# Rotary half swap in a two-block transformer kernel: four small SBUF-to-SBUF DMAs per chunk in the place of a permutation product

## The reference

```python
def apply_rope(x, ang):
    cos = jnp.cos(ang)[None, :, None, :].astype(x.dtype)
    sin = jnp.sin(ang)[None, :, None, :].astype(x.dtype)
    x1, x2 = jnp.split(x, 2, axis=-1)
    return jnp.concatenate([x1 * cos - x2 * sin, x2 * cos + x1 * sin], axis=-1)

        h = rms_norm(x, norm_mix_pre[l])
        proj = h @ w_in[l]
        qa, ka, va, qb, kb, vb = jnp.split(proj, SPLITS, axis=-1)

        qa = apply_rope(rms_norm(qa.reshape(B, S, N_HEADS_A, HEAD_DIM), q_norm_a[l]), ang_axial)
        ka = apply_rope(rms_norm(ka.reshape(B, S, N_KV_A, HEAD_DIM), k_norm_a[l]), ang_axial)
        ...
        qb = apply_rope(qb.reshape(B, S, N_HEADS_B, HEAD_DIM), ang_1d)
        kb = apply_rope(kb.reshape(B, S, N_KV_B, HEAD_DIM), ang_1d)
```

## Time and profile before

| what | value |
|---|---|
| runs | 1419.41, 1420.99, 1421.65 us; median 1420.99 us |
| the profiled execution | 1421.76 us, its span 1420.0 us |
| busy over the span | PE 96%, DVE 49%, ACT 39%, POOL 10% |
| PE (TensorE matmul) on the chain that ended last | 89% |
| the stretch of the input projection and its rotations | about 24 to 99 us from the span's start |
| the attention's steps | from 98.93 us on |

### The profile page before, as it was taken

How to read it: one execution, slowest core, us unless ns; L and a number is a source line. 1 busy time by engine, 2 the same in 40 slices (tenths; PEclk the granted TensorE clock), 3 DMA queues, 4 the chain that set the end, 5 groups by cost and what they waited for, 6 DMA issues and landing times.

```text
span 1420.0 us, 14917 instructions
## 1 busy us (share of the span) xinstructions
PE 1366.1 (96%) x6184; PEld 1092.8 (77%) x6184; DVE 689.8 (49%) x890; ACT 547.2 (39%) x736; POOL 139.5 (10%) x132
## 2 busy tenths in 40 slices
PE   7988999999999999998999999999999999999995
PEld 5664668788888888886887777788888888888874
DVE  6998764644354442226434543465443544433244
ACT  6457864523232222224224454634332322232232
POOL 3441002400000001002000000002000000000012
PEclk9999999999999999998999999999999999999997
DMA  6210003122232222231321111123222322222311
GB/s 234 65 54 1 1 1 119 60 89 90 89 107 100 90 82 91 93 120 44 119 89 60 60 60 60 60 102 107 89 89 90 105 102 89 82 90 95 120 60 60
DMA packets 20595, 117.76 MB, mean 83 GB/s; under 512 B 2480, under 2 KB 2864, under 8 KB 9904
## 3 DMA queue, kind: packets, MB, share of 16 engines
q1 hardware_dynamic: 19392, 114.57, 23.4%
q10 hardware_dynamic: 1136, 2.24, 0.5%
HBM read 114.70 MB, written 2.10 MB: 82 GB/s over the span
## 4 chain that ended last, share of the span: by engine, by line
PE 89%; DVE 7%; DMA 1%; issue 1%; ACT 1%; POOL 0%; SPq 0%; POOLq 0%; DVEq 0%
PE ps L454 87%; PE ps L649 2%; DVE rt L1218 1%; DVE w_lo L1211 1%; DMA w_raw<-weights 1%; DVE nmax L1372 1%; DVE F L1215 1%; DVE X L1211 0%; ACT w_hi L819 0%; DVE rt L1211 0%; POOL sqsum L398 0%; DVE ps L1218 0%; DVE OUT L1218 0%; DVE h_lo L1218 0%; DVE y L1211 0%
## 5 line engine op out<-in xcount | busy, mean ns | idle before, releaser
L454 PE MATMUL ps<-h_hi,w_hi 128*128 128x512 f32 x1248 | 497.7, 399 | 20.8 <-DVE w_lo L1211 10.7
L454 PE MATMUL ps<-h_hi,w_lo 128*128 128x512 f32 x1248 | 488.5, 391 | 0.0
L454 PE MATMUL ps<-h_lo,w_hi 128*128 128x512 f32 x1248 | 488.4, 391 | 0.0
L1211 DVE TENSOR_TENSOR w_lo<-w_raw,w_hi 128x2048 fp32r<-128x2048 f32 (+2 forms) x117 | 246.5, 2110 | 256.7 <-ACT w_hi L819 256.6
L454 PEld LDWEIGHTS ps<-h_hi,w_hi 128*128 128x128 f32 x1248 | 235.8, 189 | 79.4 <-issue 15.0
L819 ACT ACTIVATE w_hi<-w_raw 128x2048 fp32r<-128x2048 f32 (+2 forms) x117 | 201.4, 1723 | 196.5 <-DMA w_raw<-weights 196.4
L454 PEld LDWEIGHTS ps<-h_lo,w_hi 128*128 128x128 f32 x1248 | 236.1, 189 | 51.0 <-issue 3.1
L454 PEld LDWEIGHTS ps<-h_hi,w_lo 128*128 128x128 f32 x1248 | 235.9, 189 | 49.7
L398 POOL TENSOR_TENSOR sqsum<-sqsum,sq 128x512 f32<-128x512 f32 x62 | 89.5, 1444 | 899.6 <-ACT sq L819 897.8
L454 PE MATMUL ps<-mid_hi,w_hi 128*128 128x512 f32 x352 | 136.9, 389 | 0.0
L454 PE MATMUL ps<-mid_lo,w_hi 128*128 128x512 f32 x352 | 136.9, 389 | 0.0
(11 more groups left out here) (179 smaller groups left out, 1239.4 us busy)
## 6 DMA issues: line engine op xcount, KB each, us to landing
w_raw<-weights SPq DMA_DIRECT2D x81, 1024.0 KB, 4.8
w_raw<-weights SPq DMA_DIRECT2D x32, 704.0 KB, 4.2
out_t<-OUT SPq DMA_DIRECT2D x8, 256.0 KB, 2.0
X<-x_t SPq DMA_DIRECT2D x3, 512.0 KB, 7.5
c<-constants ACTq DMA_DIRECT2D x1, 1280.0 KB, 9.5
w_raw<-weights SPq DMA_DIRECT2D x4, 256.0 KB, 8.1
wp_raw<-weights SPq DMA_DIRECT2D x1, 1024.0 KB, 8.0
X<-x_t SPq DMA_DIRECT2D x2, 256.0 KB, 4.0
```

Source lines behind the costliest of these rows:

```text
L454: return nc.tensor.matmul(out, lhsT, rhs, start=start, stop=stop, skip_group_check=loose)
L1211: return nc.vector.tensor_tensor(out, a, b, op)
```

## The change

Each chunk that is rotated (ten of the twelve) loses its permutation product. In its place, right behind the copy of the chunk to `y`, ScalarE's queue waits for that copy to end and issues four DMAs of 32 rows by 512 fp32 (64 KB each), from `y` to a row of `PP`, each to the place of the other half. `PP` is an SBUF tensor that is free until the attention is over; four of its rows are used in turn, each with its own semaphore. VectorE's `crossed` now reads and writes that SBUF row, where it read PSUM before; the signs are in the sine table. The items of the two value chunks (transposes) stay, and so do the sums of squares.

```diff
-        def rot_bank(j):
-            return 4 + j % 2 if j < LATE1 else 7 if j != 10 else 6
+        def turned(i):
+            return PP[:, 4 + i % 4, :]
...
             def item(j):
-                if j < 0:
-                    return
                 c = ORDER1[j]
-                if j < LATE1:
-                    free_item(j - 2)
-                elif j == 10:
-                    free_item(LATE1 - 1)
-                else:
-                    free_item({LATE1: LATE1 - 2, 11: LATE1}[j])
-                if j == 0:
-                    pe.wait_ge(c1_landed, 16)
-                pe.wait_ge(evac_act, EVAC["in1", j][1])
                 if c in V1:
+                    pe.wait_ge(evac_act, EVAC["in1", j][1])
                     for b in range(NB):
...
                     mm(ps[:, HSUM_BANK, :], c1[:, C_HONE - C1_AT:C_HONE - C1_AT + P], ysq[:, n % 2, :]
                        ).then_inc(hsum_done, 1)
-                mm(ps[:, rot_bank(j), :], c1[:, C_ROT - C1_AT:C_ROT - C1_AT + P], y_of(j)).then_inc(rot_done, 1)
...
-                if s in LATE_STEPS:
-                    item(LATE_STEPS[s])
+                if s == 9:
+                    item(11)
                 pe.wait_ge(pn_ready, s + 1)
-                if s == 0:
-                    free_item(LATE1 - 2)
-                if s == 1:
-                    free_item(LATE1 - 1)
...
                 af(y_of(j), ps[:, BANK["in1", j], :], ACT.Copy).then_inc(evac_act, 1)
+                if c not in V1:
+                    i = ROPED.index(c)
+                    act.wait_ge(evac_act, EVAC["in1", j][1])
+                    for to in range(0, P, HD // 2):
+                        at = to ^ HD // 2
+                        act.dma_start(turned(i)[to:to + HD // 2, :], y_of(j)[at:at + HD // 2, :]
+                                      ).then_inc(rot_landed[i % 4], 16)
...
-                straight, crossed = (rt if j < LATE1 else rt_late)[:, 0, :], (rt if j < LATE1 else rt_late)[:, 1, :]
+                straight, crossed = (rt if j < LATE1 else rt_late)[:, 0, :], turned(i_roped)
...
-                else:
-                    dve.wait_ge(rot_done, i_roped + 1)
+                dve.wait_ge(evac_act, EVAC["in1", j][1])
                 stt(straight, y_of(j), scale, c1[:, cos:cos + S], ALU.mult, ALU.mult)
-                dve.wait_ge(rot_done, i_roped + 1)
-                m = mark(stt(crossed, ps[:, rot_bank(j), :], scale_rot, c1[:, sin:sin + S], ALU.mult, ALU.mult))
+                dve.wait_ge(rot_landed[i_roped % 4], 64 * (i_roped // 4 + 1))
+                m = mark(stt(crossed, crossed, scale_rot, c1[:, sin:sin + S], ALU.mult, ALU.mult))
...
-    for m in range(P):
-        if m % HD < half:
-            c[m + half, C_ROT + m] = -1.0
-        else:
-            c[m - half, C_ROT + m] = 1.0
...
+        sign = np.where(i % HD < half, -1.0, 1.0)[:, None]
+        c[:, cos:cos + S], c[:, sin:sin + S] = np.cos(ang), sign * np.sin(ang)
```

More of the change, by code:

```diff
@@ L66 @@
 C1_AT = C_INVC + 4 * PADW
-C_HONE, C_ROT, C_MASK = C1_AT, C1_AT + P, C1_AT + 2 * P
-C_COSA, C_SINA, C_COSB, C_SINB = (C1_AT + 4 * P + S * i for i in range(4))
+C_HONE, C_MASK = C1_AT, C1_AT + P
+C_COSA, C_SINA, C_COSB, C_SINB = (C1_AT + 3 * P + S * i for i in range(4))
 C_COLS = C_SINB + S
@@ L223, in build @@
         dve_self, act_self, pool_self = sem("dve_self"), sem("act_self"), sem("pool_self")
-        ysq_ready, rot_done, hsum_done, hvar_ready, hguess_ready, rope_done, v_ready, eps_diag, eps_ready = (
-            sem(n) for n in ("ysq_ready", "rot_done", "hsum_done", "hvar_ready", "hguess_ready", "rope_done",
+        rot_landed = [sem(f"rot_landed{i}") for i in range(4)]
+        ysq_ready, hsum_done, hvar_ready, hguess_ready, rope_done, v_ready, eps_diag, eps_ready = (
+            sem(n) for n in ("ysq_ready", "hsum_done", "hvar_ready", "hguess_ready", "rope_done",
                              "v_ready", "eps_diag", "eps_ready"))
@@ L529, in _ @@
             KS = range(KD)
[L530 to L535, removed]
-                    else:
-                        pe.wait_ge(roped, ROPED.index(ORDER1[j]) + 1)
             def item(j):
-                if j < 0:
-                    return
                 c = ORDER1[j]
-                if j < LATE1:
-                    free_item(j - 2)
-                elif j == 10:
-                    free_item(LATE1 - 1)
-                else:
-                    free_item({LATE1: LATE1 - 2, 11: LATE1}[j])
-                if j == 0:
-                    pe.wait_ge(c1_landed, 16)
-                pe.wait_ge(evac_act, EVAC["in1", j][1])
                 if c in V1:
+                    pe.wait_ge(evac_act, EVAC["in1", j][1])
                     for b in range(NB):
-                        last = nc.tensor.transpose(ps[:, rot_bank(j), b * P:(b + 1) * P],
+                        last = nc.tensor.transpose(ps[:, SIDE_BANK if j else R_BANK, b * P:(b + 1) * P],
                                                    y_of(j)[:, b * P:(b + 1) * P], ident[:, :])
                     last.then_inc(vtr_done, 1)
-                    return
-                if c in NORMED:
+                elif c in NORMED:
                     n = NORMED.index(c)
@@ L561, in item @@
                         pe.wait_ge(hvar_ready, n)
+                    else:
+                        pe.wait_ge(c1_landed, 16)
                     pe.wait_ge(ysq_ready, n + 1)
@@ L579, in beside @@
                     factor(n_mix_pre)
-                for i in (0, 1) if j == 2 else (j - 1,) if j <= LATE1 else ():
+                for i in (0, 1) if j == 2 else (j - 1,) if 2 < j <= LATE1 else ():
                     item(i)
@@ L888, in finish @@
                     for b in range(NB):
-                        last = af((VA if c == 5 else VB)[:, b, :], ps[:, rot_bank(j), b * P:(b + 1) * P], ACT.Copy,
+                        last = af((VA if c == 5 else VB)[:, b, :], ps[:, SIDE_BANK if j else R_BANK, b * P:(b + 1) * P], ACT.Copy,
                                   scale=stat[:, 3, b:b + 1])
@@ L1595, in constants @@
         ang = np.concatenate([ang.astype(np.float32)] * 4).astype(np.float64)
-        c[:, cos:cos + S], c[:, sin:sin + S] = np.cos(ang), np.sin(ang)
+        sign = np.where(i % HD < half, -1.0, 1.0)[:, None]
+        c[:, cos:cos + S], c[:, sin:sin + S] = np.cos(ang), sign * np.sin(ang)
     for g, w in enumerate(POOL_WINDOWS):
```

## The result

| | before | after |
|---|---|---|
| median of the runs, us | 1420.63 (1419.41 to 1421.65, 4 runs) | 1431.09 (1429.34 to 1432.87, 4 runs) |
| profiled execution, and its span, us | 1421.76, 1420.0 | 1430.04, 1428.3 |
| ratio to before (95% interval) | | 1.0074 (1.0058 to 1.009) |
| first `nmax`, us from the start | 98.93 | 108.20 |

The change makes the kernel slower: by 10.5 us between the medians, by 8.3 us between the two profiled executions. In the profiles it is 9.3 us late when the attention starts. The median of before is over one execution more than the table ahead of the prediction has.

A forecast was written before the change was run, and what follows sets the result against it. VectorE mainly bounds the stretch up to the first nmax, TensorE the rest. +4.7 us at the attention's start (0.86 gain included), -0.7 for late products: +4.0 on 1421.76, or 1425.0 against the median; stated 1425.5, range 1421.0 to 1431.5.

The forecast's parts named there:

- the landing rival: Landing 8.1 us after the last issue makes crossed of chunks 4, 6 and 8 wait: 1429.5 us, chance 0.08.
- the costless burst: Rival: ScalarE's queue runs ahead, bursts of 0.5 us, 1421.3 us; chance 0.18, including bursts short enough to end under 1423.8.
- the faster case: Bursts vanish and products count in full, 0.86 us at the start and 2.54 in the attention: 1417.6 us, chance 0.04.
- the walk: Chunk by chunk, lateness goes round burst, cast, GpSimd, evacuation, burst, Ln and Exp, VectorE: 4.7 us at the attention's start.
- The start: Chunk 1's removed product stands ahead of the product that VectorE's sqsum copy awaits: 0.86 us gained, sqsum at 35.9.
- The burst: Four DMA issues in ScalarE's queue, 0.47 us each plus 0.1 waiting: 2.0 us, holding up all ScalarE does behind it.
- near 0.45 us: Sign of being right: DMA rows on ScalarE's queue near 0.45 us, four in a row ten times.
- Everything 0.86 us early: The walk's first step: up to chunk 3 everything runs 0.86 us ahead of the kernel before.
- The landing: DMAs land in 2.3 us; bursts end 5 us or more ahead of their crossed, costing nothing; crossed idling on DMA contradicts.
- `crossed` from SBUF: Priced like straight; beside GpSimd it loses 0 to 1.0 us per chunk met, already counted in the walk.
- The late products: Removed products of chunks 9 and 10 in the attention's first steps: 0 to 2.54 us gain possible, 0.7 taken.
- That TensorE gives nothing back: After the projection TensorE carries the rest of the program, with no slack to give a late start back.

The follow-up runs named there:

- eight issues: The changed kernel with eight DMAs of 16 rows per burst in place of four of 32, same bytes: 1454.48 us, ratio 1.0233.
- three issues: The changed kernel with three of each burst's four issues on ScalarE's queue and the fourth on SyncE's: 1425.39 us, ratio 1.0035.
- only the bursts: The kernel before plus the ten bursts on ScalarE and VectorE's landing wait; products kept, crossed from PSUM, DMA data unused: 1434.08 us, ratio 1.0084.
- the products kept: The changed kernel with bursts on SyncE, crossed from SBUF, permutation products still computed but unused: 1421.72 us, ratio 1.0004.
- two and three issues: Two runs: the three-issue one, and the changed kernel with two issues of each burst on ScalarE, two on SyncE: 1423.53 us, ratio 1.0011.
- DMAs for three chunks: The kernel before with DMAs from SyncE replacing the products of chunks 1, 9 and 10 only: 1417.45 us, ratio 0.997.
- the burst behind: The changed kernel with each burst moved on ScalarE's queue behind the Ln, Exp and casts that follow: 1420.39 us, ratio 0.9991.
- all but chunk 8: The changed kernel with its DMAs on SyncE, chunk 8 alone keeping its product and crossing from PSUM: 1417.71 us, ratio 0.9983.
- all ten on SyncE: The changed kernel with its ten bursts issued by SyncE between weight loads, all else as in the change: 1419.05 us, ratio 0.9989.
- DMAs unused: The kernel before plus the ten bursts on SyncE, landing awaited, products used, crossed from PSUM: 1420.92 us, ratio 0.9998.

## Why the prediction was right, and where it was wrong

**Direction, rival and range held.** Slower, by the bursts on ScalarE; the landing rival, the costless burst and the faster case did not come. 1431.09 lies in the range, 0.4 us from its upper end, and that is luck in part: the end was drawn for 0.6 us an issue with a late landing added, the landing added nothing to the time, and a turn at chunk 1's keys and a long burst that the walk did not have came in its place. The central size was under half: 4.9 us forecast over the median of now, 10.5 measured.

**The start.** `sqsum` was forecast at 35.9 and came at 35.76. Shown only as a time: in the other kernels that drop chunk 1's product it lay between 35.40 and 36.46 (but for eight issues, 42.09, where ScalarE held it up), in those that keep it between 36.69 and 37.02. So the gain is there, 0.9 us by the middle of either group.

**The burst, the term that failed.** I took 0.47 us an issue, 2.0 a burst, from the distance of two issues at the start, and kept 0.83 an issue, 3.4 a burst, for the range. It was 0.61 and 2.44, once 3.46: my sign "near 0.45 us" failed. With three issues, where the burst has the length that I gave it, the median is 1.0035 of before, beside the 1.003 of the forecast, and the attention starts 6.1 us late beside 4.7. So of the 4.6 us that the first `nmax` came later than forecast, about 3.2 go with the longer burst and 1.4 with the walk itself. Its mechanism and most of its size stand; its input was 0.4 us too short, ten times. At chunks 4, 5 and 7 it was some 2 us short even at its own length of burst (3.0, 4.5, 7.2 beside 1.2, 2.6, 5.1): for chunk 4 the 2.71 us burst accounts for 0.7, and GpSimd's pair of chunk 2, 3.47 us beside VectorE and 2.69 before, for about 0.5 us.

**"Everything 0.86 us early" to chunk 3, the step at which that counted.** Chunk 3's burst held up the Ln of chunk 2 and with it the casts of chunk 1, so GpSimd was only 0.4 us early (46.21, before 46.61), while VectorE was 1.0 early. VectorE then met one key instruction less and came to its `w_lo` at 49.67, ahead of the fourth, which is the row at 50.98: 3.20 us and not 1.6. I had foreseen this for chunk 3's keys, not for chunk 1's. It made the copy of chunk 4 1.2 us late and not 0.9 early, 2.0 us off. With three issues that instruction started at 50.81, ahead of a `w_lo` at 51.20, and took 1.61; the copy came at 52.99, where the forecast puts it at 52.7 (53.58 - 0.86). In the run with only the bursts it fell behind again (`w_lo` at 50.95, the fourth at 52.25, 3.21 us). Chunk 3's burst took 2.67 us in the change, 2.69 with only the bursts and 2.06 with three issues. So 0.6 us of burst decide over a turn of 2 us.

**Chunk 4 in full.** Its Ln was forecast at 62.2 and started at 66.32, 4.1 us off: 2.0 for that turn, 0.5 for the longer burst of chunk 4, 1.5 for the 3.46 us burst of chunk 5, 0.1 the rest. From there on the walk was nearly right: lateness grew by 1.9 and 3.0 us to chunks 5 and 7, forecast 1.4 and 2.5.

**The landing.** 2.3 us were forecast, 2.0 to 2.1 came, but VectorE did wait for it once. `crossed` of chunk 4 waited 1.46 us, because VectorE was 3.0 us ahead there and the copy 1.2 behind. A `crossed` that idles on a DMA was one of my signs of being wrong, and it came: the claim that every burst ends 5 us or more ahead of its `crossed` failed at chunk 4. The 1.46 us are not in the sum of the loss: VectorE waited 5.56 us for the Ln right behind it, and would have waited that much longer.

**`crossed` from SBUF.** With GpSimd at rest its price is `straight`'s (0.69 beside 0.69 at 103.55 and 102.94), and beside GpSimd it takes up to 1.8 us. The Trainium skill ("SBUF — State Buffer", *Who interferes with whom*) has two SBUF inputs and a GpSimd reader exclude each other; the walk's turns of about 1.0 us agree. In the run with the products kept, the operand's cost is below what can be measured.

**The late products.** Taken as -0.7 of at most 2.54 us. Between the first `nmax` and the 64th the change gained nothing against before (+9.3, then +9.6 us). With two and three issues it was 0.9 and 0.7 us (+4.1 to +3.2, +6.1 to +5.4), and with DMAs for three chunks 4.1 (+0.2 to -3.8), more than the products' own length. These are single profiles, and executions of before alone range from 1415.63 to 1426.78 us; the three-chunk kernel's median, 3.3 us below before, is the firm number for both gains together.

**That TensorE gives nothing back.** Right: 9.3 us at the first `nmax`, 9.6 at the 64th, 8.3 at the end.

The Trainium skill ("DMA: Bandwidth & Descriptors", *Issuing engines are not separate DMA queues*) calls the time to initiate a DMA on the sequencer "usually small relative to the DMA itself". Here it is 0.61 us a piece beside a landing of 2.1, and for a burst 2.44: the trace does not agree for small pieces issued in a row. The same section says that initiating DMAs on several engines at once saves only the sequencer's time for it. That time is what the move to SyncE took off ScalarE, and here it is everything; where both queues issued at once, part of it was lost again (0.87 us for an issue).

## What to carry to other kernels

A DMA issue takes the time of the issuing engine's queue, in program order: in this kernel 0.6 us for each in a row. If the burst waits for the instruction just ahead of it, the engine stands still for all of it; if not, the queue issues beside the work that stands ahead, as in the run with the burst behind. So put issues on a queue where nothing urgent stands behind (SyncE here), or behind the urgent work. Ask of a burst not how busy its engine is, but what stands directly behind it and who waits for that; in a loop of engines that take turns, 0.4 us more can cost several. Replacing a product by a DMA pays where TensorE is waited for: three of ten chunks gave 0.997. That the other seven should keep their products is not shown: all but chunk 8 gave 0.9983 with nearly the same median, all ten on SyncE 0.9989.

## What was unexpected in the hardware

**The price of an issue.** 0.61 us each on ScalarE's queue and 2.41 for four on SyncE's, where those at the start took 0.33 to 0.45. An issue right behind another takes longer here: the first of a burst takes 0.51 us, those behind it 0.61, and the same weight load 0.34 alone and 0.58 behind a burst. Half the bytes changed nothing (0.63). With the other queue issuing too, an issue took 0.87. Bursts of 3.46, 2.98 and 2.71 us came between 61 and 65 us in three kernels (the change, only the bursts, three issues), beside the usual 2.44 or 2.05; in the change it is a single issue of 1.63 us. Why is open.

**TensorE's clock at the attention's start.** Take the 4 us ahead of the attention's first transposes and the 4 us behind their start. In three kernels (before, DMAs unused, three chunks) TensorE idled for 1.59, 1.59 and 1.35 us ahead, and its granted clock behind was 1.00, that is 2.4 GHz. In the other ten, the change among them, it idled for 2.33 to 3.37 us, and the clock behind was 0.50 to 0.66, most of it at 1.2 GHz; one row of four transposes then took up to 1.12 us in the place of 0.66. That the idle time brings the fall is how the rows lie, not something that a run has separated. Less work for TensorE is not needed for it: with the products kept it had all the work of before, idled 2.33 us and had a clock of 0.58. What the fall costs in the end is not shown either: all but chunk 8 has it, three chunks has not, and their medians are 1417.71 and 1417.45 us. Two things lengthen the idle time. With all but chunk 8, TensorE's last scores end 1.3 us sooner (98.51, before 99.85), but the scaling that it waits for starts only 0.5 us sooner (100.17) and takes 1.10 us beside GpSimd in the place of 0.73.
